# Turning parts of a gated linear attention layer through DRAM and VectorE instead of TensorE

## The chip, the cores and the metric

The kernel runs on one core of one Trainium2 chip. The metric is the time of the device for one execution, in microseconds (us). Engines: TensorE (PE; its weight loads are PEld), VectorE (DVE), ScalarE (ACT), GpSimd (POOL) and SyncE (SP), which here only issues DMAs.

## The reference, cut to what matters

One layer: a gated linear attention mixer (GLA) and a SwiGLU feed-forward, each behind an RMS norm, and a last RMS norm; 2048 tokens, width 1024, 4 heads with keys of 128 and values of 256, hidden width 2816.

```python
hn = rmsnorm(x, norm_mix_g)
q, k, v, r, a_low = split(hn @ w_in)
log_a = log_sigmoid(a_low @ w_a2 + b_a) / 16
# chunks of 64: scores from q, k and cumulated decays; state carried from chunk to chunk
o = scores @ v + q_fwd @ s_prev
o = rmsnorm_per_head(o) * silu(r)              # og in the kernel
h = x + o @ w_out
g, u = split(rmsnorm(h, norm_ffn_g) @ w_gu)    # its input is xf in the kernel
h = h + (silu(g) * u) @ w_down
return rmsnorm(h, final_norm_g)
```

## The kernel before

All products of two large operands are made in three passes: each operand is split into a high part (a rounded fp32r, ScalarE or GpSimd) and a low part (the rest, VectorE or GpSimd), and TensorE adds hi x hi, hi x lo and lo x hi (`three`, L733).

**Stages.** The attention stage goes by blocks of T = 512 tokens (NB = 4 blocks `b`, each of NT = 4 tiles of 128 tokens) and in a block by H = 4 heads `hd`; n = 4b + hd. After it come the feed-forward's products (from about 900 us on), which take their operands x_op from DRAM. All engines' programs are written out by hand, with semaphores; each engine does its instructions in the order of its program.

**The ring.** The weights of the attention stage come in rounds of four units of 128x512 (16 rounds a block, 3 for each head, 4 for w_out): SyncE loads pairs of units into `raw` (`load_pair`, L399, which waits until GpSimd has split the pair's units of the round before), GpSimd splits unit after unit into ring_hi and ring_lo (L660, L663), which waits until TensorE has used the unit of the round before. So SyncE and GpSimd are at most about a round ahead of TensorE. The order on SyncE in a head is: pair q, pair k (`columns`), two pairs of v and r, further loads, two more pairs of v and r.

**A head.** TensorE: `make_scores` (turns of k, then the products for past and future into banks 6 and 7), four units of v and r, the first half of the next head's q and k columns (waits for k_lo, `k_tok_done`), then it waits for the silu of r (`r_silu`) and does `use_scores`, the second half of the columns, unit 2 of the next v and r, `turn_o` and unit 3. VectorE (L1685): k_lo, mask copies into scores, scores_lo, then `under_vr` (in blocks 1 to 3, heads 0 to 2, three low parts of the x operands of the block before; in head 3 of blocks 0 to 2 the scaling of the next block's x), state_in, v_lo twice, the state, `under_o`, the root, og; then `scale_qk` of the next head and `turned_o_lo`. ScalarE: k_hi, copies of the scores, scores_hi, its part of `under_vr` (with its own stores, `result_store`), v_hi twice, silu, squares, root, decays, `turned_o_hi`. In head 3 the order on TensorE differs: there are no columns between v and r and `use_scores`.

**The turns.** TensorE turns x (normalised, xs) for the next block (`turn_next`), the gated output og of every head (`turn_o`, 8 transposes into banks 6 and 7, from where ScalarE and VectorE make oT_hi and oT_lo), and the normalised result of the block (`turn_result`, 8 transposes for each of 4 tiles, placed after each unit of v and r at the start of the next block), which ScalarE copies to xf; from xf the x operands of the feed-forward are made during the next block's heads 0 to 2. GpSimd makes sums of xf between its units (`result_sum`, L364).

**Storage.** xs, h and xf share their space with later tiles (x_stage lies in xs, xf[0] in parts 4 to 7 of oT_lo and oT_hi).

Of the kernel before, what the change touches and what calls it, by code (L numbers as in the profile page):

```python
# [5 lines left out]
P = 128  # L6
# [14 lines left out]
def gla_layer(nc, x, norm_mix_g, norm_ffn_g, w_in, w_a2, b_a, gla_norm_g, w_out, w_gu, w_down, final_norm_g, out):  # L21
# [18 lines left out]
    q_w = w_in[0, :, 0:QK].rearrange("(k p) n -> p k n", p=P)  # L40
    k_w = w_in[0, :, QK:2 * QK].rearrange("(k p) n -> p k n", p=P)
    v_w = w_in[0, :, 2 * QK:2 * QK + VD].rearrange("(k p) n -> p k n", p=P)
    r_w = w_in[0, :, 2 * QK + VD:2 * QK + 2 * VD].rearrange("(k p) n -> p k n", p=P)
    a_w = w_in[0, :, 2 * QK + 2 * VD:].rearrange("(k p) n -> p k n", p=P)
    o_w = w_out[0].rearrange("(k p) n -> p k n", p=P)
    gu_w = w_gu[0].rearrange("(k p) n -> p k n", p=P)
# [4 lines left out]
    with ExitStack() as ctx:  # L51
# [54 lines left out]
        xs = sb("xs", XS, [P, NT, D])  # L106
        h = sb("h", HH, [P, NT, D])
# [3 lines left out]
        oT_lo = sb("oT_lo", OT, [P, KV, T], F32R)  # L111
        oT_hi = sb("oT_hi", OT + 16384, [P, KV, T], F32R)
        og = sb("og", OG, [P, NT, DV])

# [46 lines left out]
        hres = nc.dram_tensor("hres", [SEQ, D], F32)  # L161
        xlate = nc.dram_tensor("xlate", [4, P, 2, T], F32)
# [6 lines left out]
        def sems(name, n):  # L169
# [25 lines left out]
                             "oT_lo_done"))  # L195
        wo_done, wo_added = sem("wo_done"), sem("wo_added")
        xs_sum, xop_hi, xop_lo = sem("xs_sum"), sem("xop_hi"), sem("xop_lo")
        xop_stored = sems("xop_stored", 3)
        xf_stored, x_in_loaded = sem("xf_stored"), sem("x_in_loaded")
# [11 lines left out]
        fin_loaded, fin_added, fin_scaled, fin_summed = (  # L211
            sem(n) for n in ("fin_loaded", "fin_added", "fin_scaled", "fin_summed"))
# [20 lines left out]
        def turn_ffn(b):  # L233
            return 2 + 2 * b if b < NB - 1 else 1 + 2 * b

# [162 lines left out]
        def _(sp):  # L398
# [13 lines left out]
            def rows(i, p, w, k, start):  # L412

                load_pair(i, p, [(raw[:, p, u, :], w[:, k + u, start:start + UNIT]) for u in range(2)])

# [59 lines left out]
            def load_late(k):  # L475

                if k == 0:
                    sp.wait_ge(xf_stored, 2 * 16)
                else:
                    sp.wait_ge(xop_lo, LATE_FROM + len(LATE) * k)  # L480
# [9 lines left out]
            def load_vr(i, hd, n):  # L490
                for p in range(2):
                    k = 4 * n + 2 * p
                    load_pair(i, p, [(raw[:, p, :, 0:DV], v_w[:, k:k + 2, hd * DV:(hd + 1) * DV]),
                                     (raw[:, p, :, DV:], r_w[:, k:k + 2, hd * DV:(hd + 1) * DV])])

            def load_out(i, n):
                half, k2 = divmod(n, KV // 2)
                rows(i, n % 2, o_w, 2 * k2, half * HALF)
# [1640 lines left out]
```

## Time and profile before

| | us |
|---|---|
| median of 3 runs (2193.34 to 2200.28) | 2199.96 |
| the profiled execution | 2198.29 |
| its span, first to last instruction | 2196.6 |

One execution is shown by the profile. Times in it are us from the span's start unless marked ns. A line such as `TENSOR_TENSOR k_lo<-ps,k_hi` names what is written and what is read; the number in square brackets is the time for which the engine had stood idle, and what ended that. SPq is SyncE's queue, with the time it takes to issue.

### The profile page before, as it was taken

What the parts mean: (1) busy time and instruction counts of PE and PEld (TensorE: products, weight loads), DVE (VectorE), ACT (ScalarE), POOL (GpSimd) and SP (SyncE); (2) the same over time, 40 slices, a digit from 0 to 9 for tenths busy, and PEclk for the clock granted to TensorE, in tenths of its full rate; (3) what the DMA queues carried; (4) which work ended last, traced back from release to release, by engine and by line L of the source; (5) the groups of instructions that cost most, each with busy time, mean ns of one, the idle gap of its engine ahead of it and who ended that gap; (6) DMA issues with size and microseconds to landing.
All of it is one profiled execution on the core that took longest, in us unless ns stands there. A gap on an engine that the chain in (4) does not pass through costs nothing.

```text
span 2196.6 us, 27842 instructions
## 1 busy us (share of the span) xinstructions
PE 2149.8 (98%) x9922; PEld 1776.9 (81%) x9922; DVE 1384.1 (63%) x1800; ACT 823.6 (37%) x1461; POOL 1630.0 (74%) x1294
## 2 busy tenths in 40 slices
PE   8999999999999999999999998999999999999997
PEld 6888888778878888778888877888888878888885
DVE  6445644554455453378787855757667567978786
ACT  4333433343344333344444433443434422142223
POOL 7646675667566765788888878888888887878784
PEclk9999999999999999999999999999999999999999
DMA  6222354335433655745545458443434588759782
GB/s 187 77 67 87 121 186 121 119 114 189 123 131 110 200 162 201 259 158 201 182 175 192 161 206 344 151 166 135 171 132 174 206 308 311 282 214 359 262 320 105
DMA packets 225545, 404.75 MB, mean 184 GB/s; under 512 B 17184, under 2 KB 156448, under 8 KB 216448
## 3 DMA queue, kind: packets, MB, share of 16 engines
q1 hardware_dynamic: 190448, 360.44, 46.0%
q10 hardware_dynamic: 34960, 42.54, 5.8%
q8 instruction: 79, 1.29, 0.2%
q14 instruction: 58, 0.48, 0.1%
HBM read 273.94 MB, written 128.97 MB: 183 GB/s over the span
## 4 chain that ended last, share of the span: by engine, by line
PE 60%; DVE 3%; POOL 2%; issue 1%; DMA 1%; ACT 1%; SPq 0%; ACTq 0%; POOLq 0%; DVEq 0%
PE ps L735 20%; PE ps L737 20%; PE ps L736 20%; DVE acc L2012 1%; DMA x_op<-xop 1%; POOL ring_lo L663 1%; POOL ring_hi L660 0%; POOL w_op L672 0%; DMA raw<-in_gla_w_out 0%; DVE xs L1540 0%; PE ps L870 0%; DVE acc L1979 0%; SPq L473 0%; DMA raw<-in_gla_w_in 0%; DVE p_sum L2012 0%
## 5 line engine op out<-in xcount | busy, mean ns | idle before, releaser
L672 POOL TENSOR_TENSOR w_op<-w_raw,w_op 128x512 fp32r<-128x512 f32 x330 | 482.7, 1474 | 112.3 <-ACT w_op L1085 109.2
L735 PE MATMUL ps<-x_op,w_op 128*128 128x512 f32 x1232 | 480.9, 390 | 9.2 <-DMA x_op<-xop 3.3
L737 PE MATMUL ps<-x_op,w_op 128*128 128x512 f32 x1232 | 480.1, 390 | 0.0
L736 PE MATMUL ps<-x_op,w_op 128*128 128x512 f32 x1232 | 479.8, 389 | 0.0
L660 POOL TENSOR_SCALAR ring_hi<-raw 128x512 fp32r<-128x512 f32 x256 | 177.3, 693 | 293.8 <-issue 168.2
L663 POOL TENSOR_TENSOR ring_lo<-raw,ring_hi 128x512 fp32r<-128x512 f32 x256 | 351.7, 1374 | 21.3
L1085 ACT ACTIVATE w_op<-w_raw 128x512 fp32r<-128x512 f32 x330 | 202.6, 626 | 378.2 <-POOL w_raw L690 147.6
L735 PEld LDWEIGHTS ps<-x_op,w_op 128*128 128x128 f32 x1232 | 231.7, 188 | 59.5 <-issue 9.1
L737 PEld LDWEIGHTS ps<-x_op,w_op 128*128 128x128 f32 x1232 | 231.6, 188 | 48.4
L736 PEld LDWEIGHTS ps<-x_op,w_op 128*128 128x128 f32 x1232 | 231.8, 188 | 47.8
L735 PE MATMUL ps<-w_op,hid 128*128 128x512 f32 x616 | 240.8, 391 | 3.3 <-DVE acc L2012 0.9
L737 PE MATMUL ps<-w_op,hid 128*128 128x512 f32 x616 | 239.7, 389 | 0.0
L736 PE MATMUL ps<-w_op,hid 128*128 128x512 f32 x616 | 239.7, 389 | 0.0
L735 PE MATMUL ps<-ring_hi,xT_hi 128*128 128x512 f32 x512 | 203.5, 398 | 4.5 <-POOL ring_lo L663 4.5
L737 PE MATMUL ps<-ring_hi,xT_lo 128*128 128x512 f32 x512 | 200.3, 391 | 0.0
L736 PE MATMUL ps<-ring_lo,xT_hi 128*128 128x512 f32 x512 | 199.7, 390 | 0.0
L672 POOL TENSOR_TENSOR w_op<-w_t,w_op 128x512 fp32r<-128x512 f32 x112 | 169.1, 1509 | 29.3 <-ACT w_op L1085 29.3
L2012 DVE TENSOR_TENSOR acc<-acc,ps 128x512 f32<-128x512 f32 x224 | 145.8, 682 | 52.6 <-PE ps L737 51.2
L1085 ACT ACTIVATE w_op<-w_t 128x512 fp32r<-128x512 f32 x112 | 70.6, 630 | 209.4 <-POOL w_t L684 165.7
L735 PEld LDWEIGHTS ps<-w_op,hid 128*128 128x128 f32 x616 | 115.6, 188 | 31.8 <-issue 4.9
L737 PEld LDWEIGHTS ps<-w_op,hid 128*128 128x128 f32 x616 | 115.6, 188 | 24.1
L736 PEld LDWEIGHTS ps<-w_op,hid 128*128 128x128 f32 x616 | 115.6, 188 | 23.6
(206 smaller groups left out, 3992.3 us busy)
## 6 DMA issues: line engine op xcount, KB each, us to landing
hop<-stage SPq DMA_DIRECT2D x154, 512.0 KB, 2.9
hid<-hop SPq DMA_DIRECT2D x70, 1024.0 KB, 9.6
raw<-in_gla_w_in SPq DMA_DIRECT2D x192, 256.0 KB, 3.3
w_raw<-in_ffn_w_gu SPq DMA_DIRECT2D x176, 256.0 KB, 4.0
w_raw<-in_ffn_w_down SPq DMA_DIRECT2D x88, 256.0 KB, 4.5
xop<-x_stage ACTq DMA_DIRECT2D x42, 512.0 KB, 3.5
x_op<-xop SPq DMA_DIRECT2D x36, 512.0 KB, 8.6
raw<-in_gla_w_out SPq DMA_DIRECT2D x64, 256.0 KB, 3.1
```

Of the source, the lines that this page charges most:

```text
L660: pool.tensor_scalar(ring_hi[:, u, :], raw[:, p, u % 2, :], 1.0, 0.0, ALU.mult, ALU.add).then_inc(unit_hi, 1)
L663: pool.tensor_tensor(ring_lo[:, u, :], raw[:, p, u % 2, :], ring_hi[:, u, :].bitcast(F32), ALU.subtract).then_inc(unit_split[u], 1)
L672: pool.tensor_tensor(shaped(q, tile[:, 1, :]), source(q, i), shaped(q, tile[:, 0, :]).bitcast(F32), ALU.subtract).then_inc(op_ready[i], 1)
L735: pe.matmul(out, l_hi, r_hi, start=first, stop=False, skip_group_check=more)
L736: pe.matmul(out, l_hi, r_lo, start=False, stop=False, skip_group_check=more)
L737: return pe.matmul(out, l_lo, r_hi, start=False, stop=last, skip_group_check=more)
L1085: return act.activation(dst, src, ACT.Copy)
L2012: ins = dve.tensor_tensor(dst, dst, bank, ALU.add)
```

## The change

It changes four things.

- og of heads 0 to 2 of each block is no longer turned by TensorE. SyncE stores og in DRAM (`og_kept`), loads it back in four DMAs so that the 32 rows of a block lie on 32 partitions and the four quarters of the columns on the four groups of partitions, and VectorE turns blocks of 32x32 in two instructions into oT (f32, in the place of oT_lo). ScalarE makes oT_hi in the next head, after the copies of the scores, and VectorE oT_lo after scores_lo. Head 3 is turned by TensorE as before.
- xs of blocks 0 to 2 (the normalised result) takes the same way in two halves of 256 tokens, eight VectorE instructions a half, into xf. `turn_result` and ScalarE's copies remain for block 3 alone.
- Columns of x and of og are dealt out in another order, so that what VectorE's turns give fits: partition p, part k is column 8p + k of x and 2p + j of og's head. The weights' rows are loaded in that order, and TensorE's remaining transposes read every eighth (xs) or second (og) column.
- Order: the waits of `make_scores` change, `store_h` moves from head 0 to head 1, `load_x` between the two last pairs of head 3, and at the kernel's very end two steps of the norm's squares, roots and scalings change places. Some semaphores are merged.

```diff
-    q_w = w_in[0, :, 0:QK].rearrange("(k p) n -> p k n", p=P)
+    q_w = w_in[0, :, 0:QK].rearrange("(p k) n -> p k n", p=P)
...
+    o_w = w_out[0].rearrange("(h p j) n -> h j p n", p=P, j=2)
+    gu_w = w_gu[0].rearrange("(p k) n -> p k n", p=P)
...
+            def store_xs(b, half):
+                two = slice(2 * half, 2 * half + 2)
+                sp.wait_ge(xs_ready, NT * turn_ffn(b) + two.stop)
+                sp.dma_start(xs_kept[:, :].rearrange("(t p) c -> p t c", p=P)[:, two, :], xs[:, two, :])\
+                    .then_inc(xs_stored, 16)
+
+            def load_xs(b, half):
+                sp.wait_ge(xs_stored, 16 * (2 * b + half + 1))
+                by_32 = xs_kept[:, :].rearrange("(m s) (i c) -> i s m c", s=32, i=4)
+                tokens = slice(half * T // 64, (half + 1) * T // 64)
+                for i in range(4):
+                    sp.dma_start(xs_by_32[32 * i:32 * i + 32, tokens, :], by_32[i, :, tokens, :])\
+                        .then_inc(xs_back[half], 16)
...
+            def store_og(b, hd):
+                sp.wait_ge(og_done, NT * (b * H + hd + 1))
+                sp.dma_start(og_kept[:, :].rearrange("(t p) c -> p t c", p=P), og[:, :, :]).then_inc(og_stored, 16)
+
+            def load_og(b, hd):
+                sp.wait_ge(og_stored, 16 * (b * (H - 1) + hd + 1))
+                by_32 = og_kept[:, :].rearrange("(m s) (i c) -> i s m c", s=32, i=4)
+                for i in range(4):
+                    sp.dma_start(og_by_32[32 * i:32 * i + 32, :, :], by_32[i]).then_inc(og_loaded, 16)
...
                 for hd in range(H):
                     i = b * ROUNDS + 3 * hd
+                    if hd >= 2:
+                        store_og(b, hd - 2)
                     columns(i, 0, q_w, hd * DK)
+                    if hd >= 2:
+                        load_og(b, hd - 2)
                     columns(i, 1, k_w, hd * DK)
+                    if hd == 1 and b > 0:
+                        store_h(b - 1)
                     load_vr(i + 1, hd, 0)
...
-                    if hd == H - 1 and 0 < b < NB - 1:
-                        wait_operands(b)
-                        load_x(b + 1)
-                    load_vr(i + 2, hd, 1)
+                    def between():
+                        if hd == H - 1 and 0 < b < NB - 1:
+                            wait_operands(b)
+                            load_x(b + 1)
+                        if hd == 0 and b > 0:
+                            load_xs(b - 1, 0)
+                            store_xs(b - 1, 1)
+
+                    if hd == 0 and b > 0:
+                        store_xs(b - 1, 0)
+                    load_vr(i + 2, hd, 1, between)
+                    if hd == 0 and b > 0:
+                        load_xs(b - 1, 1)
...
-                    if hd == 0 and b > 0:
-                        store_h(b - 1)
+                store_og(b, H - 2)
+                load_og(b, H - 2)
...
                     ins = pe.transpose(ps[:, bank0 + k // 4, (k % 4) * P:(k % 4 + 1) * P],
-                                       xs[:, t, k * P:(k + 1) * P], ident[:, :])
+                                       xs[:, t, k::KD], ident[:, :])
...
-                if n > 0:
-                    pe.wait_ge(oT_lo_done, 2 * n)
-                if n > 0 and n % H == 0:
-                    pe.wait_ge(xf_done, 2 * NT * (n // H) - 1)
+                if n % H > 0:
+                    pe.wait_ge(og_done, NT * n)
+                elif n > 0:
+                    pe.wait_ge(oT_lo_done, (H + 1) * (n // H))
...
                     vr_unit(i + 4, 0, 2)
-                    turn_o(n)
                     vr_unit(i + 4, 0, 3)
...
                     for u in range(4):
                         vr_unit(first + ROUNDS + 1, 0, u)
-                        turn_result(b, u)
...
                 act.activation(scores[CHUNK:, :, CHUNK:], past[CHUNK:, :, CHUNK:], ACT.Copy).then_inc(past_copied, 1)
+                if hd > 0:
+                    turned_o_hi(b, hd - 1)
                 act.wait_ge(scores_ready, 2 * (n + 1))
...
                 split_lo(scores_lo[:, :, :], scores[:, :, :], scores_hi[:, :, :]).then_inc(scores_split, 1)
+                if hd > 0:
+                    turned_o_lo(b, hd - 1)
+                elif b > 0:
+                    turn_x_blocks(b - 1, 1)
                 under_vr()
...
+            def turn_x_blocks(b, half):
+
+                dve.wait_ge(xs_back[half], 16 * 4 * (b + 1))
+                tokens = slice(half * T // 2, (half + 1) * T // 2)
+                by_k = xs_by_32[:, half * T // 64:(half + 1) * T // 64, :].rearrange("p m (r k) -> p k m r", k=KD)
+                for k in range(KD):
+                    ins = dve.transpose(xf[0][k // 4][:, k % 4, tokens].rearrange("p (m s) -> p m s", s=32),
+                                        by_k[:, k, :, :])
+                    if k % 2 == 1:
+                        ins.then_inc(xf_done, 1)
+
+            def turn_o_blocks(b, hd):
+
+                dve.wait_ge(og_loaded, 16 * 4 * ((H - 1) * b + hd + 1))
+                for j in range(2):
+                    ins = dve.transpose(oT[:, 2 * hd + j, :].rearrange("p (m s) -> p m s", s=32),
+                                        og_by_32[:, :, j::2])
+                ins.then_inc(oT_blocks, 1)
...
                 for hd in range(H - 1):
                     head(b, hd, operands_under_vr(hd), operands_under_o(hd))
                     scale_qk(b * H + hd + 1)
-                    turned_o_lo(b, hd)
+                    turn_o_blocks(b, hd)
...
                 norm_result(b)
                 if more:
                     scale_qk((b + 1) * H)
+                    turn_x_blocks(b, 0)
```

## Rows read from the trace of the kernel before

**Rows 1.** The page: busy time, share of the span and instructions of each engine.

```profile
PE 2149.8 (98%) x9922; PEld 1776.9 (81%) x9922; DVE 1384.1 (63%) x1800; ACT 823.6 (37%) x1461; POOL 1630.0 (74%) x1294
```

**Rows 2.** Waits of TensorE, 10 to 900 us: for whom, sum, times, longest.

```profile
PE ps L735 <- POOL ring_lo L663: 7.8, 13, 2.2
...
PE ps L841 <- ACT xf L1139: 1.0, 3, 0.3
```

**Rows 3.** The chain of waits: start, length, a group of 8 transposes each.

```profile
702.55 0.87 PE ps L765 x8
...
833.46 0.87 PE ps L878 x8
```

**Rows 4.** Timeline of SyncE's queue: pairs of weight loads, start and length.

```profile
303.66 0.88 SPq L405 DMA_DIRECT2D raw<-in_gla_w_in  x2
...
308.82 2.25 SPq L405 DMA_DIRECT2D raw<-in_gla_w_in  x2
...
345.46 0.88 SPq L405 DMA_DIRECT2D raw<-in_gla_w_in  x2
...
349.38 0.92 SPq L405 DMA_DIRECT2D raw<-in_gla_w_in  x2
...
164.68 0.88 SPq L405 DMA_DIRECT2D raw<-in_gla_w_in  x2
```

**Rows 5.** DMA issues: queue, count, KB each, median us from issue to landing.

```profile
raw<-in_gla_w_in SPq DMA_DIRECT2D x192, 256.0 KB, 3.3
...
xop<-x_stage ACTq DMA_DIRECT2D x42, 512.0 KB, 3.5
...
hres<-h SPq DMA_DIRECT2D x16, 512.0 KB, 5.1
```

**Rows 6.** Timeline of VectorE, block 1, heads 0 to 2.

```profile
299.72 1.66 DVE L1729 SCALAR_TENSOR_TENSOR og<-ps,rstd,r_gate 128x256 f32<-128x256 f32 x4
...
303.08 0.68 DVE L1617 TENSOR_TENSOR qk_scaled<-ps,ef 128x512 f32<-128x512 f32 x1
...
308.93 0.69 DVE L1516 TENSOR_TENSOR k_lo<-ps,k_hi 128x512 fp32r<-128x512 f32 x1 [2.33 <-ACT k_hi L1085]
...
315.96 1.39 DVE L1516 TENSOR_TENSOR x_stage<-xf,x_stage 128x512 fp32r<-128x512 f32 x1 [2.27 <-ACT x_stage L1085]
...
320.22 0.69 DVE L1516 TENSOR_TENSOR v_lo<-ps,v_hi 128x512 fp32r<-128x512 f32 x1 [0.55 <-ACT v_hi L1085]
...
350.76 0.69 DVE L1516 TENSOR_TENSOR k_lo<-ps,k_hi 128x512 fp32r<-128x512 f32 x1 [2.36 <-ACT k_hi L1085]
```

**Rows 7.** Timeline of ScalarE, block 1, head 1: the silu.

```profile
323.64 1.03 ACT L1210 ACTIVATE r_gate<-ps 128x1024 f32<-128x1024 f32 x1
```

**Rows 8.** Timeline of TensorE: starts of use_scores, block 1 head 1, block 0 head 3.

```profile
326.19 0.28 PE L735 MATMUL ps<-v_hi,k_hi 128*128 128x256 f32 x1
...
182.16 0.39 PE L735 MATMUL ps<-v_hi,k_hi 128*128 128x256 f32 x1 [0.24 <-DVE v_lo L1516]
```

**Rows 9.** Timeline of VectorE, block 0, head 1, then head 3.

```profile
100.18 0.69 DVE L1516 TENSOR_TENSOR v_lo<-ps,v_hi 128x512 fp32r<-128x512 f32 x1 [7.35 <-ACT v_hi L1085]
...
169.95 0.69 DVE L1516 TENSOR_TENSOR k_lo<-ps,k_hi 128x512 fp32r<-128x512 f32 x1 [2.34 <-ACT k_hi L1085]
...
181.41 0.69 DVE L1516 TENSOR_TENSOR v_lo<-ps,v_hi 128x512 fp32r<-128x512 f32 x1
```

**Rows 10.** Timelines of VectorE and GpSimd, border of blocks 0 and 1.

```profile
256.15 3.78 DVE L1540 SCALAR_TENSOR_TENSOR xs<-h,rstd,g_ffn 128x1024 f32<-128x1024 f32 x2
...
279.69 0.69 DVE L1516 TENSOR_TENSOR v_lo<-ps,v_hi 128x512 fp32r<-128x512 f32 x1 [3.73 <-ACT v_hi L1085]
...
267.89 1.27 POOL L373 TENSOR_TENSOR x_sum<-xf,xf 128x512 f32<-128x512 f32 x1
```

**Rows 11.** TensorE's timeline, then a stretch: busy by engine, granted clock, DMA.

```profile
1349.26 0.47 PE L735 MATMUL ps<-x_op,w_op 128*128 128x512 f32 x1 [3.26 <-DMA x_op<-xop]
...
1350.00:1354.00 4.00, 3.85 (x10) 2.63 (x9) 3.75 (x3) 2.79 (x5) 4.00 (x4) 0.60 1.02 417
```

## What the change will do to the time

> **What bounds the kernel now.** I read the page's busy shares first: TensorE is busy for 2149.8 of 2196.6 us [rows 1]. In a kernel like this an instruction taken off TensorE is worth its own time, and a new wait of TensorE costs its whole length; what the other engines do is free as long as it stays beside TensorE. Then I read TensorE's waits in the attention stage, where all that is changed lies: the largest sum by releaser is 7.8 us, for GpSimd's ring_lo, and the wait for the turned result (xf) is 1.0 us in three times [rows 2]. So TensorE bounds the stage, and the other engines are close behind it. How close, the timelines of one head show: before the products of head 1 in block 1, ScalarE ends the silu (r_gate) at 323.64 + 1.03 = 324.67 [rows 7] and TensorE starts at 326.19 [rows 8], a margin of 1.5 us; VectorE waited 0.55 us for v_hi ahead of v_lo [rows 6]. The margin of the chain VectorE k_lo, scores_lo, x_stage, state_in, v_lo, ScalarE silu is thus 2.1 us in the heads that also prepare x operands. In head 3 it is nothing: TensorE already waits 0.24 us for v_lo [rows 8].
>
> **What goes.** 12 groups of 8 transposes of og (heads 0 to 2 of four blocks) and 12 groups of xs (the result of blocks 0 to 2) leave TensorE. Such a group takes 0.87 us in the chain of waits [rows 3]: 24 x 0.87 = 20.9 us. With the groups of xs goes the wait for xf, 1.0 us [rows 2]. Sum: 21.9 us gained. ScalarE's copies to xf go too; they lay beside TensorE and give nothing of their own.
>
> **What comes, head by head.** og of head n now goes to DRAM, comes back as blocks of 32 rows, and VectorE turns it in two instructions. VectorE stands in order, and turn_o_blocks is put between scale_qk of the next head and that head's k_lo: while it waits for og_loaded, k_lo, the mask copies, scores_lo, the x operands, state_in and v_lo of the next head stand behind it; ScalarE's scores_hi and silu wait for those, and TensorE's use_scores for the silu. When does og come back? Both transfers are in SyncE's queue, among the weight loads, which it issues only as GpSimd frees the raw tile. In block 1 og is made by 299.72 + 1.66 = 301.4 [rows 6], but SyncE issues the pair of loads that stands ahead of the store at 303.66, until 304.5 [rows 4]. A store of 512 KB lands after 3.5 us (xop<-x_stage, pieces of 1 KB as here) [rows 5]: 308.0. The next pair of loads goes at 308.82; with two issues of 0.44 us it ends at 309.7 [rows 4], and the four loads of og behind it take 1.8 us to issue, until 311.5. Their landing is in no row, since no load here has pieces of 256 B: the bounds are 3.3 us (weight loads, 256 KB) and 5.1 us (hres<-h, 512 KB) [rows 5]. I take 3.3, the nearest in size and in place in the queue: 314.8. The two block turns of 128x512 are in no row either; one pass of 128x512 is 0.68 us [rows 6], so 1.4 us, with twice that as the upper bound. VectorE comes to k_lo at 316.2 instead of 308.93 [rows 6], 7.3 us later, having stood idle since 303.8. Off that go the margins of 2.1 us, and 0.87 us come on, because TensorE itself arrives earlier: a stall of 6.1 us in head 1. For head 2 the same count from the loads at 345.46 and 349.38 [rows 4] gives 349.38 + 0.92 + 1.8 + 3.3 + 1.4 = 356.8 against 350.76 [rows 6], 6.0 us late and a stall of 4.8. For head 3 (block 0) the store goes at 164.68 + 0.88 = 165.6 [rows 4], is in DRAM at 169.1, and there is no pair of loads between: 169.1 + 1.8 + 3.3 + 1.4 = 175.6 against k_lo at 169.95 [rows 9], 5.6 us late, with no margin: 6.2 us with the 0.87 and less the 0.24 already there. Blocks 1 to 3 have the first two, blocks 0 to 2 the third (head 3 of blocks 0 to 2 has the next block's squares and scaling in that chain, k_lo at 169.95 to v_lo at 181.41 [rows 9]): 3 x (6.1 + 4.8 + 6.2) = 51.3 us. The lower half oT_lo moves behind scores_lo; it lies in VectorE's waits for ScalarE (2.27 us ahead of one x_stage [rows 6]) and costs nothing; without that cover, 1.3 us a head.
>
> In heads 1 and 2 of block 0 and head 3 of block 3 nothing stands in that chain, and VectorE waits 7.35 us ahead of v_lo [rows 9]. The same delay of 6 to 7 us just fits: 0.5 us each, 1.5 us.
>
> **The clock.** Nine stalls of 5 to 6 us are new to TensorE. Where it stood idle for 3.26 us ahead of 1349.26, the granted clock of 1350 to 1354 is 0.60, so that part of it was at the lower level, 1.2 GHz [rows 11]; 4 x 0.4 = 1.6 us lost. I take 9 x 1.6 = 14.4 us, with 0 as the other bound.
>
> **The block's border.** xs takes the same way by halves. Its second half is ready at 256.15 + 3.78 = 259.9 [rows 10]; store 3.5, four issues 1.8, landing 3.3 give 268.5, and VectorE then has 8 turns of 128x256 in each half, 16 in all; by half a pass of 0.68 with its start, some 0.4 us each, 3.3 us a half, to 272 or, at twice that, 275. x_sum on GpSimd, at 267.89 before [rows 10], and v_lo, with a wait of 3.73 us ahead of it [rows 10], come behind that, while TensorE arrives 3.8 us earlier. So the border lies between 0 and 3 us: 1.5 us x 3 = 4.5 us. store_h moves to head 1 and load_x between two loads; h and x are wanted much later, so nothing. Other row order of the weights: same pieces, same bytes, nothing. The order of the last squares and scalings: within 1 us either way, nothing.
>
> **Sum.** -21.9 + 51.3 + 1.5 + 4.5 + 14.4 = +49.8 us, on the profiled execution's own 2198.3 us (span 2196.6; the median of the runs is 2200.0): 2248 us.
>
> **A rule weighed.** TensorE's remaining 20 groups of xs now read every eighth column, and so do VectorE's turns of x, a step of 32 bytes; every row of a transpose before has adjoining columns, at 0.87 us a group [rows 3]. I take that price, the only one there is, and twice it as the upper bound: 20 x 0.87 = 17.4 us. The Trainium skill, "SBUF — State Buffer", section "Door 1: The DMA port swizzle", says that consecutive accesses run at full rate only if at least two fall in the same line of 16 bytes; by that rule it would be the upper bound, and the 8 byte step of og free. No row of before shows such a step. The Trainium skill, "DMA: Bandwidth & Descriptors", section "Specifications", wants at least 512 B in a transfer for line rate; og's loads have 256 B, which would put their landing towards 5.1 us, 9 x 1.8 = 16 us more.
>
> **The rivals.** (a) The strided reads cost double: a mechanism of its own on top of the forecast, 2248 + 17 = 2265 us. Chance 0.15. (b) SyncE is ahead of its place in the rows and the store goes out as soon as og is made, at 301.4: all comes back 3 us sooner, the stalls shrink to 3.1, 1.8 and 3.2 us, no gap reaches the 3.26 us of rows 11, and the clock is taken to stay up: 24.3 + 1.5 + 4.5 - 21.9 = +8 us, 2206 us. Against it: the raw tile frees at GpSimd's pace, behind TensorE. Chance 0.10. (c) Faster: og is back before it is missed. That wants it turned within 2.1 - 0.9 = 1.2 us after 308.93, so landed by 308.8 in block 1, 6 us before my count; or the chain behind k_lo shortens by as much. Then only the removal is left: 2198.3 - 21.9 = 2176 us. For it: no row times such loads, and VectorE's waits of 7.35 us [rows 9] show how much cover some heads have. Against it: it needs a store and a load in 7.4 us, with two pairs of weight loads in the same queue. The gain must outweigh nine stalls, so it decides at 21.9 / 9 = 2.4 us a head. Chance 0.15. (d) That the transposes aren't really gone, or leave their time behind on TensorE, I give nothing: they are separate instructions with a time of their own in the chain.
>
> **How the numbers follow.** The forecast has 0.60. Its own range: without the clock's and the border's price 2229, with more margin in the chain some 2222; with landings of 5.1 us (+16) and the border at 3 us (+4.5) 2269. The range for 8 in 10 is 2200 to 2275 and leaves out rival (c) and the ends. Runs of before agree within 0.3%, so 6.6 us is what can be told from no change. Faster 0.16 (rival c and a little of b), same 0.05 (the rest of b, up to 2206), slower 0.79.
>
> **What would show it.** In the profile of the changed kernel: 160 transposes from xs and 32 from og on TensorE. VectorE idle for 10 us or more ahead of its block turn of og, released by a DMA og_by_32<-og_kept that SyncE issued right behind the next pair of weight loads. TensorE's waits for DVE v_lo and ACT r_gate in the heads named, 5 to 6 us each, some 50 us in sum, and slices with a clock under 1.0 behind them. Wrong if VectorE's wait ends within 2 us of the old start of k_lo, if TensorE's waits in the stage stay under 25 us in sum, or if a group of 8 strided transposes takes more than 1 us.

## The result and the profile after

| | us | ratio to before, 95% interval |
|---|---|---|
| before, median of 4 runs beside it (2193.34 to 2200.28) | 2198.41 | |
| after, median of 4 runs (2282.24 to 2286.07) | 2283.14 | 1.0395 [1.0382, 1.0408] |
| span of the profiled execution after | 2281.1 | |

The change costs 84.7 us. The forecast had the direction and the mechanism (2248 us, slower), but the time lies 8 us above its range. The first part of the page of after, to be held against [rows 1]:

```profile
PE 2154.9 (94%) x9730; PEld 1778.7 (78%) x9730; DVE 1425.7 (63%) x1860; ACT 809.5 (35%) x1425; POOL 1633.7 (72%) x1294
```

192 instructions have left TensorE, and still it is busy for 5 us longer: it ran at a lower clock. The waits of TensorE from 10 to 900 us (for whom, sum, times, longest) answer to [rows 2]; there the largest sum was 7.8 us:

```profile
PE ps L793 <- POOL ring_lo L721: 30.8, 15, 7.5
PE ps L793 <- DVE v_lo L1578: 26.8, 3, 9.9
PE ps L793 <- ACT r_gate L1264: 26.3, 6, 6.3
```

Two stretches, up to the first transposes of the last result and from there on (length; busy time of TensorE, its weight loads, VectorE, ScalarE, GpSimd; granted clock, DMA share, GB/s), in after:

```profile
20.00:996.40 976.40, 879.19 (x4124) 730.22 (x4124) 486.41 (x772) 318.94 (x544) 572.90 (x546) 0.95 0.50 151
996.40:2281.00 1284.60, 1263.84 (x5564) 1041.96 (x5564) 927.25 (x1063) 479.84 (x861) 1052.31 (x727) 1.00 0.58 216
```

The kernel before comes to the same point at 906.7 us, with 1289.9 us behind it. So the attention stage is 89.8 us longer: TensorE's idle time grows from 13.0 to 97.2 us, and its busy time grows by 5.6 us although 24 groups of 0.87 us left it. The rest of the kernel is 5.3 us shorter. (The expectations below were written with 1289.4 and 4.8 us, half a microsecond off.)

One stall, in block 1, head 1: SyncE's queue, then VectorE, then TensorE, as in [rows 4], [rows 6] and [rows 8] (start, length, instruction; in brackets the idle time before it and what ended it):

```profile
320.30 0.47 SPq L535 DMA_DIRECT2D og_kept<-og  x1
324.53 0.92 SPq L425 DMA_DIRECT2D raw<-in_gla_w_in  x2
325.49 2.09 SPq L541 DMA_DIRECT2D og_by<-og_kept  x4
```

```profile
315.43 1.66 DVE L1795 SCALAR_TENSOR_TENSOR og<-ps,rstd,r_gate 128x256 f32<-128x256 f32 x4
...
330.85 1.31 DVE L1814 STREAM_TRANSPOSE oT<-og_by 128x512 f32<-128x512 f32 x2 [11.36 <-DMA og_by<-og_kept]
332.08 0.65 DVE L1578 TENSOR_TENSOR k_lo<-ps,k_hi 128x512 fp32r<-128x512 f32 x1
```

```profile
346.00 0.58 PE L793 MATMUL ps<-v_hi,k_hi 128*128 128x256 f32 x1 [4.83 <-ACT r_gate L1264]
```

og is made at 317.09; VectorE waits 11.36 us for its way through DRAM and comes to k_lo 15.0 us after og. The forecast had 14.8 (301.4 to 316.2). A landing of 3.3 us (327.58 to 330.85) and 1.31 us for both block turns are what was assumed. TensorE has 160 transposes of xs and 32 of og, as the forecast's signs asked. All nine stalls stand where they were forecast: 4.8, 6.1 and 6.3 us in head 1 of blocks 1 to 3, 4.5, 4.5 and 6.9 in head 2, 7.4, 9.5 and 9.9 in head 3 of blocks 0 to 2, in sum 59.9 us.

The border of blocks 0 and 1, SyncE's queue of after:

```profile
265.56 1.81 SPq L525 DMA_DIRECT2D xs_by<-xs_kept  x4
267.42 0.45 SPq L517 DMA_DIRECT2D xs_kept<-xs  x1
267.97 1.59 SPq L425 DMA_DIRECT2D raw<-in_gla_w_in  x2
275.89 1.81 SPq L525 DMA_DIRECT2D xs_by<-xs_kept  x4
277.80 5.75 SPq L425 DMA_DIRECT2D raw<-in_gla_w_in  x4
```

VectorE and GpSimd there, against [rows 10]:

```profile
282.92 4.51 DVE L1805 STREAM_TRANSPOSE xf<-xs_by 128x256 f32<-128x256 f32 x8 [2.20 <-DMA xs_by<-xs_kept]
```

```profile
278.17 0.62 POOL L718 TENSOR_SCALAR ring_hi<-raw 128x512 fp32r<-128x512 f32 x1 [7.05 <-DMA raw<-in_gla_w_in]
...
287.50 1.62 POOL L393 TENSOR_TENSOR x_sum<-xf,xf 128x512 f32<-128x512 f32 x1 [4.95 <-DVE xf L1805]
```

and TensorE's three waits of that border:

```profile
280.19 0.50 PE L793 MATMUL ps<-ring_hi,xT_hi 128*128 128x512 f32 x1 [2.30 <-POOL ring_lo L721]
291.95 0.77 PE L793 MATMUL ps<-xT_hi,ring_hi 128*128 128x512 f32 x1 [4.42 <-POOL ring_lo L721]
303.18 0.50 PE L793 MATMUL ps<-ring_hi,xT_hi 128*128 128x512 f32 x1 [2.33 <-POOL ring_lo L721]
```

This is the part that the forecast got wrong. SyncE can't load the second half before its store has landed, 8.5 us after its issue (267.42 to 275.89). The pair of weights that it had issued right behind that store (267.97 to 269.56) landed late too. The trace, asked for this pair alone:

```profile
DMA to landing us min/median/max: 7.9/8.7/9.6
```

The median of all such loads is 3.3 us. GpSimd stood idle for 7.05 us until the pair was there, and TensorE's first wait, 2.30 us, is for what GpSimd made of it. Then GpSimd's first sum waits for xf until 287.5 with the next units of the ring behind it: the second wait, 4.42 us. The third comes while GpSimd works from 287.5 on without a gap, still catching up. Three borders have 9.1, 10.0 and 10.2 us of such waits, 29.3 us in sum. The forecast had 4.5.

### The profile page after: what moved, and what is told of

Read it like the earlier page. It is cut to its first block, busy times and chain, and to the rows that moved or that the text cites. A ratio compares the mean times of both kernels' runs of the same rounds, so it can differ in the third digit from the quotient of the medians.

```text
span 2281.1 us, 27532 instructions
## 1 busy us (share of the span) xinstructions
PE 2154.9 (94%) x9730; PEld 1778.7 (78%) x9730; DVE 1425.7 (63%) x1860; ACT 809.5 (35%) x1425; POOL 1633.7 (72%) x1294
## 4 chain that ended last, share of the span: by engine, by line
PE 69%; DMA 9%; DVE 8%; POOL 5%; ACT 4%; issue 3%; SPq 2%; ACTq 0%; POOLq 0%; DVEq 0%
PE ps L793 22%; PE ps L794 22%; PE ps L795 22%; POOL ring_lo L721 3%; DMA og_by<-og_kept 2%; DMA og_kept<-og 2%; DMA xop<-x_stage 1%; POOL ring_hi L718 1%; PE ps L924 1%; DMA raw<-in_gla_w_in 1%; DVE xs L1602 1%; DVE acc L2102 1%; ACT junk L1147 1%; SPq L541 1%; DMA raw<-in_gla_w_out 1%
## 5 line engine op out<-in xcount | busy, mean ns | idle before, releaser
L793 PE MATMUL ps<-ring_hi,xT_hi 128*128 128x512 f32 x512 | 203.9, 398 | 10.2 <-POOL ring_lo L721 10.2
```

The lines of the kernel that those rows point to most:

```text
L793: pe.matmul(out, l_hi, r_hi, start=first, stop=False, skip_group_check=more)
```

## The experiments

All times are medians, beside runs of the kernel before on the same chip (medians 2196.6 to 2198.3). "The order alone" is the run order_only. The first four take the change apart.

**order_only.** Both detours undone, all else as changed:

```diff
-                    turn_o_blocks(b, hd)
+                    turned_o_lo(b, hd)
...
                     scale_qk((b + 1) * H)
-                    turn_x_blocks(b, 0)
```

> The changed kernel with both detours undone: og and xs are turned by TensorE again, at the old places, but in the new order of columns (strides of 8 and 32 bytes in 128 + 128 + the first transposes, weights' rows reordered), with store_h, load_x and the end of the kernel as changed. Theory (my forecast's): all that is left costs nothing, so it runs like the kernel before, and gives back what the trace of after shows in the last stage (1289.4 us before, 1284.6 us after, from the first transposes of the last result on): 2193 to 2199 us, no wait of TensorE over 2.5 us in the attention stage. Rival (strides of more than 16 bytes at half speed): 52 groups of xs x 0.87 us more, about 2240 us.

Measured: 2190.7 us, 0.9971 [0.9959, 0.9983]. TensorE's transposes of xs and og, all with a stride in this run (count, busy time, mean ns of one):

```profile
L810 PE MATMUL ps<-ident,xs 128*128 128x128 f32 x256 | 33.9, 275 | 5.1 <-DVE xs L1595 5.0
L923 PE MATMUL ps<-ident,og 128*128 128x128 f32 x128 | 17.8, 281 | 0.0
```

and the same in the kernel before, with adjoining columns:

```profile
L765 PE MATMUL ps<-ident,xs 128*128 128x128 f32 x256 | 33.4, 273 | 5.1 <-DVE xs L1540 5.0
L878 PE MATMUL ps<-ident,og 128*128 128x128 f32 x128 | 16.6, 272 | 0.0
```

The step of 32 bytes has 275 ns each against 273, the step of 8 bytes 281 against 272: 0.5 and 1.2 us in the whole kernel, next to nothing, and rival (a) falls. (256 transposes are 32 groups and not the 52 of the expectation, so the rival stood for some 2198 + 28 = 2226 us. It falls all the same.) The expected 2193 to 2199 us was missed too: the order by itself makes the kernel 6.7 us faster. In the traces some 2 us of it lie behind the last product (below) and 4 us in the attention stage, whose end moves from 906.7 to 902.7 while the waits for ring_lo fall from 7.8 to 3.6 us. Which of the moved loads and stores does that was not tried.

**og_dram.** Only og through DRAM; xs is turned by TensorE, with ScalarE's copies:

```diff
                     for u in range(4):
                         vr_unit(first + ROUNDS + 1, 0, u)
+                        turn_result(b, u)
...
-                    turn_x_blocks(b, 0)
```

> The changed kernel with only og through DRAM; xs is turned by TensorE and copied by ScalarE as before. Theory (the trace of after read by its waits): nine stalls of 59.9 us in sum and the 2.6 us in the last head stay, 10.4 us of transposes are gone, the clock costs about 0.36 us for each us of idle time (30.7 us more of busy time beside 84.2 us more of waits in after), 4.8 us less in the last stage: 2198 + 62.5 + 22.5 - 10.4 - 4.8 = 2268 us, and no wait for ring_lo at the blocks' borders over 2.5 us. Rival (the two detours disturb each other, and much of the nine stalls is due to the traffic and the late start that xs leaves): 2235 us or less, stalls under 4 us each.

Measured: 2257.3 us, 1.0276 [1.0261, 1.0291]. The stalls are those of after (7.3 in block 0, 5.4, 4.9 and 9.7 in block 1), no wait at a border is over 1.0 us. The detour of og costs 66.6 us over the order alone. My estimate was 11 us too high: about 4 us of that are the clock (18.4 us for the 22.5 taken, see the step by step account below) and 2 the order (6.7 us for the 4.8 taken); the rest isn't assigned.

**xs_dram.** Only xs through DRAM; og is turned by TensorE:

```diff
                     vr_unit(i + 4, 0, 2)
+                    turn_o(n)
                     vr_unit(i + 4, 0, 3)
```

> The changed kernel with only xs through DRAM; og is turned by TensorE in every head as before. Theory (read by the waits of after): the 29.3 us of waits for ring_lo at three borders stay, 10.4 us of transposes and 1.0 us of waits for xf are gone, the clock costs 0.36 us for each us, 4.8 us less in the last stage: 2198 + 29.3 + 10.5 - 11.4 - 4.8 = 2222 us. Rival (my forecast's: the border costs 1.5 us each, and the ring runs dry only because og's stalls and transfers had put it behind): 2198 - 11.4 + 4.5 - 4.8 = 2186 us, faster than before.

Measured: 2217.2 us, 1.0090 [1.0075, 1.0105], 26.5 us over the order alone, with waits of 1.9, 7.1 and 1.7 us at the first border. The rival that held the forecast's border right falls: the border is expensive without any of og's stalls. The parts add up: 2190.7 + 66.6 + 26.5 = 2283.8 us against 2283.1 measured, so the two detours hardly touch one another.

**og_late.** Is it the transfer or the place of VectorE's wait? og through DRAM, the turn later:

```diff
-                    turn_o_blocks(b, hd)
...
+                    if t == 2 and 0 < hd < H - 1:
+                        turn_o_blocks(b, hd - 1)
                     dve.wait_ge(state_in_done, NT * n + t + 1)
                     dve.wait_ge(ds_done, NT * n + 2 * (t // 2) + 2)
...
-                pe.wait_ge(oT_lo_done, (H + 1) * b + H - 1)
+                pe.wait_ge(oT_lo_done, (H + 1) * b + H - 2)
```

> As the run with only og through DRAM, but VectorE's block turn stands later: in heads 1 and 2 ahead of its third wait for the state's products, in head 3 behind scores_lo; oT_hi and oT_lo later too, and TensorE waits for the third head's part only ahead of unit 4 of w_out. Theory (the stalls come from the place of VectorE's wait alone, the transfers are harmless): no wait for v_lo or r_gate over 1 us, granted clock back to 0.99 and more, 2198 - 10.4 - 4.8 = 2183 us, up to 2190. Rival (the transfers of og and SyncE's waits for them hold up the weights, too, or TensorE is held by GpSimd anyway): waits for ring_lo of 20 us and more, 2205 us or more.

Measured: 2199.9 us, 1.0016 [1.0006, 1.0027], between the expected 2183 to 2190 and the rival's 2205. Every wait for r_gate over 0.9 us is gone and 57 of og_dram's 66.6 us with them. SyncE's order of loads and stores is the same in both; the turn moved, with ScalarE's and VectorE's hi and lo parts and one wait of TensorE. So most of the stalls come from where VectorE waits. Not all was said by that. Waits for v_lo of 1.9 to 2.7 us stay in head 3, where the turn stands ahead of the scaling, and in block 3 two for ring_lo of 5.4 and 3.7 us:

```profile
759.18 2.41 SPq L541 DMA_DIRECT2D og_by<-og_kept  x4
761.69 36.89 SPq L425 DMA_DIRECT2D raw<-in_gla_w_in  x10
```

```profile
771.47 0.62 POOL L711 TENSOR_SCALAR ring_hi<-raw 128x512 fp32r<-128x512 f32 x1 [6.12 <-DMA raw<-in_gla_w_in]
```

SyncE's k columns stand behind its wait for og's store, which in block 3 has the feed-forward's first weights ahead of it (issued at 752.60, landed 6.6 us later). They were issued from 761.69 on, and GpSimd could use them at 771.47.

**og_fill.** What does the clock take? og_dram, with products that nobody reads in the gaps:

```diff
+            def fill(count):
+                for _ in range(count):
+                    pe.matmul(ps[:, 1, :], xT_hi[:, 0, 0:P], xT_hi[:, 0, :], start=True, stop=True)
...
+                    if hd > 0 and b > 0:
+                        fill(20)
                     pe.wait_ge(r_silu, n + 1)
...
+                if b < NB - 1:
+                    fill(30)
                 use_scores(n, None)
```

> As the run with only og through DRAM (2257.3 us), but TensorE does products that nobody reads while it would stand idle: 20 of 128x512 ahead of its wait for the silu in heads 1 and 2 of blocks 1 to 3, 30 ahead of the products of head 3 in blocks 0 to 2, at 0.228 us each 4.6 and 6.8 us, less than the stalls they lie in. Theory (a stall costs its length and then half speed: in that run the stretch behind the stall of 5.44 us has a granted clock of 0.50 for 3.5 us, and the attention stage 20 us more of busy time): the same ends of VectorE's chain, but no low clock behind it, 2237 us, up to 2243 where a part of the gap stays idle; granted clock 0.99. Rival (the clock falls by something else, by the DMA traffic or the transposes' place, or the low clock is not on the path): 2254 us or more, clock 0.98.

Measured: 2248.9 us, 1.0232 [1.0217, 1.0247], 8.4 us less by useless work alone, 12 us short of the forecast of 20. The clock granted over a whole run is 0.993 to 0.996, where og_dram's runs have 0.980 to 0.983. Two stretches in og_dram (the 5.44 us of idle time end at 339.5), columns as above:

```profile
334.00:339.50 5.50, 0.08 (x1) 0.00 (x0) 3.05 (x4) 3.33 (x5) 5.33 (x6) 0.80 0.99 290
339.50:343.00 3.50, 3.47 (x14) 3.29 (x15) 3.31 (x5) 1.01 (x2) 0.63 (x1) 0.50 0.57 166
343.00:347.00 4.00, 4.00 (x19) 3.34 (x18) 0.06 (x1) 0.04 (x1) 0.00 (x0) 0.86 0.00 0
```

and in og_fill (TensorE alone), where the same gap has shrunk to 1.07 us:

```profile
336.90:341.00 4.10, 4.10 (x24) 1.00 0.46 143
```

The mechanism holds: behind a stall TensorE runs at the lower level, 1.2 GHz, here 3.5 us at 0.50 and part of the next 4 us, 3.5 x 0.50 + 4 x 0.14 = 2.3 us lost. The size fell short, for one, because the filler didn't close the gaps: 3.84 us stay in head 3 of block 1, with a clock of 0.61 in the 4 us behind it. By an estimate from the traces (attention stage's busy time of 920.5 us less 210 fillers at 0.228 us, against 883.3) 10.7 of the clock's 18.4 us came back.

**og_load_x.** Why is head 3's stall 9.5 us in block 1 and 7.4 in block 0?

```diff
-                    load_vr(i + 2, hd, 1, between)
+                    if hd == H - 1 and 0 < b < NB - 1:
+                        wait_operands(b)
+                        load_x(b + 1)
+                    load_vr(i + 2, hd, 1)
```

> As the run with only og through DRAM (2257.3 us), but the load of the next block's x is issued again ahead of both last pairs of head 3, as in the kernel before. Theory (og's store in head 3 of blocks 1 and 2 lands 2 us later than in block 0, 5.8 against 3.9 us, because 2 MB of x stand ahead of it in the queues): the waits for v_lo of 9.7 and 10.1 us come down to the 7.3 us of block 0, about 5 to 6 us less, 2252 us. Rival (head 3's stall in blocks 1 and 2 is longer for another reason, the row of SyncE's issues or the x operands of the block before): they stay at 9.5 us and more, 2257 us.

Measured: 2259.6 us, 1.0283 [1.0267, 1.0298]: no gain. The edit moved x's load only from 402.9 to 399.3, og's store went out 3.6 us earlier too and took 7.3 us to land (404.4 to 411.7; 6.4 in og_dram), and new waits for ring_lo of 1.7 and 2.7 us came up. Head 3's waits did fall, from 9.7 to 9.0 and from 10.1 to 6.6 us, but TensorE only came to them later: in block 2, where the wait fell most, the store took 8.2 us. The expected number failed. That x's 2 MB delay the store stays likely but unshown: in after the loads follow the store's issue by 4.3 us in block 0 (164.06 to 168.38), where no x is loaded, and by 6.3 us in block 1 (413.34 to 419.60).

**xs_sp.** Is the border SyncE's order?

```diff
-                            load_xs(b - 1, 0)
-                            store_xs(b - 1, 1)
...
                     if hd == 0 and b > 0:
-                        load_xs(b - 1, 1)
+                        load_xs(b - 1, 0)
+                        store_xs(b - 1, 1)
```

(the second half's load now stands ahead of the k columns of head 1).

> As the run with only xs through DRAM (2217.2 us), with SyncE's order at the border changed: both pairs of weights first, then load of the first half and store of the second, and the load of the second half behind the next pair. Theory (two causes lie in a border: SyncE and its queues hold up the raw weights, 1.9 and 1.7 us; GpSimd's first sum waits for xf and holds the ring, 7.1 us): the two short waits go, the long one stays at 6 us or more, 2217.2 - 3 x 3.6 x 1.3 = 2203 us. Rival A (all of it is SyncE's order): the long wait goes too, 2190 us or less. Rival B (it is xf's way as such, and a later issue of the half makes it later): the long wait grows by as much as the short ones shrink, 2217 us.

Measured: 2223.9 us, 1.0113 [1.0096, 1.0130], 6.7 us more. The intervals just touch, but the traces agree: TensorE's waits for ring_lo in the stage are 41.7 us in sum for 35.3. Rival B: the first short wait goes, and the long one grows from 7.1 to 11.6 us:

```profile
288.23 0.77 PE L787 MATMUL ps<-xT_hi,ring_hi 128*128 128x512 f32 x1 [11.58 <-POOL ring_lo L715]
```

The weights were not what ended last; the turned second half was. Its store, with one more pair of weights in front of it, took 11.1 us to land, where it took 8.9 in xs_dram.

**xs_sum.** GpSimd's sums two units later:

```diff
-            SUM_AFTER = {(2, 3): 0, (3, 1): 1, (3, 3): 2, (4, 1): 3, (4, 3): 4, (5, 1): 5,
+            SUM_AFTER = {(3, 1): 0, (3, 3): 1, (4, 1): 2, (4, 3): 3, (5, 1): 4, (5, 3): 5,
```

> As the run with only xs through DRAM (2217.2 us), but GpSimd makes each of its first six sums of xf two units of weights later (the first behind unit 1 of round 3, not behind unit 3 of round 2). Theory (the long wait at the border, 7.1 us, is the ring standing behind the first sum, which waits for the turned second half): that wait goes, and TensorE then meets the silu, which ended at 289.5 there, 4 us after it would be ready for it; the short waits of 1.9 and 1.7 us stay: 3 us less a border, 2217 - 3 x 3 x 1.3 = 2205 us, up to 2210. Rival (the silu and v_lo behind VectorE's turns are as late as the ring, so that a wait only changes its name): 2215 us or more.

Measured: 2206.8 us, 1.0047 [1.0030, 1.0063], 10.4 us less than xs_dram. The wait of 7.1 us is gone, and the silu is next, as expected:

```profile
289.61 0.55 PE L787 MATMUL ps<-v_hi,k_hi 128*128 128x256 f32 x1 [3.34 <-ACT r_gate L1255]
```

**xs_sp_sum.** Both edits:

> SyncE's order of the run xs_sp (2223.9 us, waits of 11.6, 10.1 and 10.7 us for ring_lo behind the first sum) with the later sums of xs_sum. Theory (SyncE's new order had made the second half later by 4 us and so the sum; with the sum out of the way the early weights count): no wait for ring_lo over 2.5 us, but the silu is late by the same 4 us, so about as xs_sum or up to 5 us more: 2205 to 2212 us. Rival (weights and sums were both free beside VectorE's 9 us of turns): 2218 us or more.

Measured: 2214.1 us, 1.0073 [1.0059, 1.0088], between what was expected and the rival. The waits for ring_lo are 5.4 us in sum, and three for the silu are 9.8, 8.7 and 9.4 us, longer than the 4 us expected beyond xs_sum's. At the border three things wait for the second half: the sum, what VectorE has behind its turns (v_lo, and by it the silu), and the weights, which SyncE issues behind the wait for its store.

**og_late2 and og_late3.** Can the detour of og be worth anything? og_late2 takes both remains of og_late away (it also moves the feed-forward's first weights behind og's loads, and the hi and lo parts of head 3):

```diff
-                        load_og(b, hd - 2)
                     columns(i, 1, k_w, hd * DK)
+                    if hd >= 2:
+                        load_og(b, hd - 2)
...
                 if hd == H - 1:
                     gate_r(n)
+                    turn_o_blocks(b, hd - 1)
```

> As the run with the block turns later (2199.9 us), with three things more: the four loads of og stand behind the pair of k columns (behind the second pair of w_out in head 3), the loads of the feed-forward's first weights in block 3 stand behind them, and in head 3 VectorE turns og behind the gating of r. Theory (what was left there came from SyncE standing behind its own store while weights were due, 5.4 and 3.7 us of waits for ring_lo in block 3, and from the turn in head 3 ahead of v_lo, 6.8 us): all waits under 1.5 us, 2190.7 for the order alone less 10.4 of transposes = 2180 us, up to 2186. Rival (DRAM traffic of og slows GpSimd's and VectorE's work or the raw loads wherever it stands): 2192 us or more, no gain over the order alone.

Measured: 2191.4 us, 0.9979 [0.9968, 0.9990], faster than before and no better than the order alone; the expected 2180 to 2186 us failed. TensorE's waits there, 10 to 1060 us, three of their rows:

```profile
PE ps L787 <- POOL ring_lo L715: 8.8, 10, 2.4
...
PE ps L817 <- DVE xT_lo L1583: 3.8, 3, 1.3
PE ps L787 <- DVE v_lo L1583: 2.3, 3, 1.5
```

The order alone has 3.6, none and 0.9 us. That is 10.4 us more, as much as the transposes had given.

og_late3 moves one low part:

```diff
                     turned_lo(b + 1, 0, 4)
+                turned_o_lo(b, H - 2)
+                if more:
                     turned_lo(b + 1, 1, 4)
```

> As og_late2 (2191.4 us, no better than the order of columns alone, 2190.7), but the low part of the third head's og stands behind the low part of the first turned tile of the next block's x, not ahead of it. Theory (the 10.4 us of transposes are given back in small waits: 3.8 us for xT_lo, 5.2 us more for ring_lo, since GpSimd splits and sums without a gap there, 1.4 us more for v_lo): the 3.8 us go, the rest stays, 2187.6 us. Rival (TensorE is bound there by another engine as a whole, and a wait that goes comes back at the next place): 2190 us or more, other waits longer by as much.

Measured: 2189.1 us, 0.9957 [0.9944, 0.9970]. The waits for xT_lo went, and small ones for oT_lo (1.5 us in sum) and v_lo came. It is the fastest complete kernel here, but its interval overlaps with that of the order alone (2190.7): the detour of og gives some 2 of its 10.4 us (1.7 by the medians, 3.1 by the ratios to the kernel before), if anything.

**order_old_tail.** The order alone, with the last squares, roots and scalings as before:

```diff
-            for j in range(3):
+            for j in range(4):
...
-            square_of(1, 3, 0)
-            square_of(1, 3, 1)
-            root_of(1, 2)
```

> The order of columns alone (2190.7 us) with the last squares, roots and scalings of the kernel before. Theory (behind the last product there were 12.9 us before and 11.1 us after the change): 1.8 us more, 2192.5 us, 12.9 us behind the last product. Rival (the end's order is worth all of the 4 us that the last stage has lost): 2194.5 us or more.

Measured: 2193.4 us, 0.9978 [0.9969, 0.9987], 2.7 us over the order alone (1.5 by the ratios) where 1.8 were expected; the intervals overlap, so the times alone prove nothing. The traces do show it: behind the last product there are 12.8 us here as before, and 10.7 in the order alone.

**few_og_turns and few_turns.** Are TensorE's transposes worth their time? The order alone with most of them left out (the first edit in both runs, the second in few_turns alone; the result is then not the layer's):

```diff
-                    for t in range(NT):
+                    for t in range(NT) if n % H == H - 1 else (NT - 1,):
                         ins = pe.transpose(ps[:, 6 + j, t * P:(t + 1) * P], og[:, t, j::2], ident[:, :])
...
-                turn_rows(t, result_banks(b, t))
+                turn_rows(t, result_banks(b, t), range(KD) if b == NB - 1 else (KD - 1,))
```

> The order of columns alone (2190.7 us), with 6 of the 8 transposes of og left out in heads 0 to 2 of every block (the rest of the turned tile is whatever stood in the bank, so the result isn't the reference's); no DMA and nothing on VectorE is added. 12 x 6/8 x 0.87 = 7.8 us of TensorE's work go. Theory (an instruction off TensorE is worth its time): 2183 us. Rival (what og_late2 showed: GpSimd's ring and VectorE's chain hold TensorE there, and give back about as much in waits for ring_lo and v_lo): 2187 us or more, with 4 us and more of new waits.

> As few_og_turns, and of the transposes of xs in blocks 0 to 2 only one of 8 is done, too (again the result isn't the reference's): 12 x 7/8 x 0.87 = 9.1 us more. Theory: 2190.7 - 16.9 = 2174 us. Rival: 2182 us or more, the difference in waits for ring_lo at the borders, where GpSimd's first sum then stands ahead of TensorE.

Measured: 2183.9 us, 0.9939 [0.9926, 0.9953], and 2175.0 us, 0.9900 [0.9886, 0.9913]: 6.8 and 15.7 us less than the order alone, where 7.8 and 16.9 were to be had. Nearly all of their time is real. (The profiled run of few_og_turns, the slowest of its five at 2188.6 us, has 3.0 us more of waits for ring_lo than the order alone, so GpSimd isn't far behind.) TensorE was free to use the time, and what og_late2 and og_late3 lose again, their detour brings in itself. Which part of it, VectorE's added turns, ScalarE's hi parts, SyncE's added issues or their traffic, wasn't separated.

## Why the forecast missed, step by step

- **What bounds the kernel.** Right: a transpose off TensorE is worth its 0.87 us a group (15.7 of 16.9 us in few_turns), and a wait costs its length. Strides cost TensorE next to nothing, as the sum took it. The rule weighed, that of the Trainium skill, "SBUF — State Buffer", section "Door 1: The DMA port swizzle", lets each access that crosses to a new line of 16 bytes pay a penalty; it gives no size, and the factor of two was my own bound. On TensorE the measurement says no for the step of 32 bytes (275 ns against 273); the step of 8 bytes, free by the rule, is 9 ns dearer (281 against 272).
- **The nine stalls.** Right in place, cause and, in heads 1 and 2, size: 33.1 us measured (4.8 + 4.5 + 6.1 + 4.5 + 6.3 + 6.9) for 32.7 forecast. That the sum fits so well is partly luck: single stalls were off by 1.3 us down (block 1, head 1) and 2.1 us up (block 3, head 2). In head 3 it was 26.8 for 18.6: block 0's 7.4 was forecast at 6.2, blocks 1 and 2 had 9.5 and 9.9. The count for head 3 was made in block 0 and carried to blocks where og's store lands 2 us later (6.2 us for 4.3). 2 MB of x stand in the queues ahead of it there, a load that the change moved and the forecast costed at nothing; that it is the cause isn't shown (og_load_x).
- **The heads that just fit.** Nothing in block 0, 2.6 us in head 3 of block 3, for 1.5 forecast. Right in sum.
- **The clock.** The mechanism was right, the term was sized too small. Busy time in the attention stage, with the removed groups at 0.87 us added back and set against the 875.3 us of the order alone, is up by 18.4 us in og_dram, 7.3 in xs_dram, 24.8 in after. That is 2.0 us for each of og's nine stalls where 1.6 was taken from one wait of 3.26 us [rows 11], and 7.3 us for the border's waits, which had no clock term at all.
- **The block's border.** This step failed: 29.3 us for 4.5. It followed one chain (store, loads, 16 turns, sum, v_lo) and sized it too short: from the second half's readiness to xf there are 20.7 us (266.7 to 287.4) where 12 to 15 were counted. The store was taken at 3.5 us from one of 512 KB; this one has 1 MB, with 1 MB of loads just ahead of it, and took 8.5. The loads took 7.0 us from the first issue to VectorE's start (275.9 to 282.9) for 5.1, and the eight turns of a half 4.5 us for 3.3. And it left out what stands behind: the weights issued behind the store, which landed after 7.9 and 9.6 us for 3.3, and on GpSimd the ring behind the sum. xs_sum shows the second of these alone to be worth 10.4 us; the first wasn't tried by itself.
- **What was costed at nothing.** The order of the rest was worth 6.7 us the other way.
- **Sum.** In place of the forecast's +49.8: -20.9 and -1.0 for what goes, +59.9 and +2.6 for og's stalls, +1.1 for a wait for k_lo, +29.3 for the borders, +24.8 for the clock, -6.7 for the order: +89.1, against 84.7 measured; the 4.4 us between them are not assigned. With 29.3 at the border and its 7.3 of clock alone the forecast would have been 2280 us.
- **The rivals.** (b) SyncE ahead of its place: no, it issued og's store 3.2 us after og was made, as forecast. (c) og back before it is missed: no, and og_late shows what brings most of that time back, not a faster transfer but a wait at another place. The range was too narrow because the border's upper bound was carried from one chain only.

## What to carry to other kernels

When work moves from a saturated engine to another by way of memory, put the receiving engine's wait where the engine stands idle anyway, not where the data could first be used: og's detour cost 66.6 us with the wait at one place and 9.2 us at another, with SyncE's order unchanged. With its loads moved as well it cost nothing measurable, but even then the 10.4 us of transposes that it took off TensorE were used up. Count for each added DMA not only its own chain but what stands behind it on the issuing queue and on each engine that waits for its result, and take a landing time from a transfer of the same size under the same traffic; the transfers that follow it in the queue land later as well. Try what rides along with a change by itself: here the reordering alone was a gain of 6.7 us, hidden under a loss of 92.

## What the runs showed of the hardware

- Behind an idle time of 5.4 us TensorE's granted clock was 0.50 for 3.5 us and 0.86 in the next 4 us; behind one of 1.07 us it stayed at 1.00.
- Transfers issued close together landed later. At the first border the store of 1 MB took 8.5 us and the pair of weights issued right behind it 7.9 and 9.6 us, where the median of these weights is 3.3 us; in xs_sp, with one more pair in front of it, the store took 11.1 us.
- Loads of 128 KB in pieces of 256 B (og_by) landed after 3.4 us, those of 256 KB of weights after 3.3 us, so twice the bytes in the same time. The Trainium skill, "DMA: Bandwidth & Descriptors", section "Specifications", wants 512 B or more for line rate. The landing of 3.3 us that the forecast took held, and not the 5.1 us that it drew from this; no load of 128 KB in larger pieces is in these traces, so the price of small pieces by itself was not measured. The rows of the DMA issues of after (KB each, median us from issue to landing):

```profile
og_kept<-og SPq DMA_DIRECT2D x12, 512.0 KB, 4.3
og_by<-og_kept SPq DMA_DIRECT2D x48, 128.0 KB, 3.4
xs_kept<-xs SPq DMA_DIRECT2D x6, 1024.0 KB, 6.2
xs_by<-xs_kept SPq DMA_DIRECT2D x24, 256.0 KB, 5.0
```

- VectorE's two block turns of 128x512 with a step of 8 bytes took 1.31 us, 0.66 each, and its eight of 128x256 with a step of 32 bytes 4.51 us, 0.56 each, so more than half for half the elements. Whether that is the step or a fixed start was not tried.
